# Gate and up projections as seven Strassen block products for eight, with the output and feed-forward stages arranged around them

## What is computed

```python
h = h + y @ w_out                                  # y: 1024 wide
hn = rmsnorm(h, norm_ffn_g)
gate, up = split(hn @ w_ffn_up)                    # 2 x 2816 features
gate = dwconv(gate, conv_ffn_w, conv_ffn_b)        # 3 taps over tokens t-1, t, t+1
h = h + (silu(gate) * up) @ w_ffn_down             # 2816 -> 1024
return h[16:]
```

## Time and profile before

| | us |
|---|---|
| median of 3 runs | 1465.31 |
| the profiled execution | 1464.26 |
| its span, first to last instruction | 1462.4 |
| input, recurrence, attention, first half of the output stage | 655.65 |
| second half of the output stage, to the first feed-forward matmul | 61.85 |
| feed-forward stage | 744.9 |
| one turn of the feed-forward loop | 66.74 |

### The profile page before, as it was taken

The page is one execution under the profiler, slowest core; times in us unless marked ns, Lnnn a source line. Parts: engine busy times, 40 slices in busy tenths (PEclk is TensorE's granted clock), DMA queues, the critical chain, the costliest instruction groups (busy, mean ns, idle before and its releaser), DMA issues.

```text
span 1462.4 us, 17247 instructions
## 1 busy us (share of the span) xinstructions
PE 1374.9 (94%) x6918; PEld 1150.0 (79%) x6918; DVE 728.3 (50%) x1002; ACT 527.3 (36%) x698; POOL 240.8 (16%) x133
## 2 busy tenths in 40 slices
PE   6989996799999987899799999999999999999998
PEld 5988995566666655587688989888888889898886
DVE  6767749577777751636333343424333332424243
ACT  6577624466666661525330212121111202121200
POOL 0000124000000000344221303122121213032100
PEclk9999899699999995899899999999999999999999
DMA  5101100000000032210120102021111102020103
GB/s 196 52 26 50 52 1 1 0 2 8 9 9 15 9 100 91 64 38 1 58 86 29 58 29 86 14 72 43 43 43 43 57 29 63 23 86 14 44 1 115
DMA packets 21094, 64.32 MB, mean 44 GB/s; under 512 B 5442, under 2 KB 6146, under 8 KB 18228
## 3 DMA queue, kind: packets, MB, share of 16 engines
q1 hardware_dynamic: 20676, 63.36, 12.7%
q10 hardware_dynamic: 368, 0.27, 0.1%
HBM read 59.20 MB, written 4.23 MB: 43 GB/s over the span
## 4 chain that ended last, share of the span: by engine, by line
PE 50%; DVE 0%; ACT 0%; issue 0%; DVEq 0%
PE banks L100 17%; PE banks L101 17%; PE banks L102 17%; DVE a_l L1867 0%; DVE ffn_act L1863 0%; ACT a_h L1829 0%; DVE h L1876 0%; DVEq L1862 0%
## 5 line engine op out<-in xcount | busy, mean ns | idle before, releaser
L100 PE MATMUL banks<-hn_h,up_h 128*128 128x342 f32 (+1 forms) x880 | 309.0, 351 | 1.7 <-PEq L1483 1.7
L101 PE MATMUL banks<-hn_l,up_h 128*128 128x342 f32 (+1 forms) x880 | 308.6, 351 | 0.0
L102 PE MATMUL banks<-hn_h,up_l 128*128 128x342 f32 (+1 forms) x880 | 308.0, 350 | 0.0
L100 PEld LDWEIGHTS banks<-hn_h,up_h 128*128 128x128 f32 x880 | 166.8, 190 | 17.1 <-POOL up_l L1509 1.8
L101 PEld LDWEIGHTS banks<-hn_l,up_h 128*128 128x128 f32 x880 | 167.1, 190 | 15.3
L102 PEld LDWEIGHTS banks<-hn_h,up_l 128*128 128x128 f32 x880 | 166.6, 189 | 15.6
L1876 DVE TENSOR_TENSOR h<-banks,h 128x512 f32<-128x512 f32 x176 | 121.7, 692 | 114.6 <-PE banks L102 114.6
L100 PE MATMUL banks<-dn_h,a_h 128*128 128x512 f32 x352 | 137.8, 392 | 3.7 <-DVE a_l L1867 3.7
L102 PE MATMUL banks<-dn_h,a_l 128*128 128x512 f32 x352 | 137.7, 391 | 0.0
L101 PE MATMUL banks<-dn_l,a_h 128*128 128x512 f32 x352 | 137.7, 391 | 0.0
L1794 POOL TENSOR_TENSOR dn_l<-dn_raw,dn_h 128x1024 fp32r<-128x1024 f32 x22 | 52.9, 2403 | 480.3 <-ACT dn_h L1827 480.3
(11 more groups left out here) (257 smaller groups left out, 2485.7 us busy)
## 6 DMA issues: line engine op xcount, KB each, us to landing
up_raw<-in_w_up SPq DMA_DIRECT2D x22, 1024.0 KB, 4.9
dn_raw<-in_w_down SPq DMA_DIRECT2D x22, 512.0 KB, 3.5
win_raw<-in_w_in SPq DMA_DIRECT2D x11, 512.0 KB, 3.3
x_tm<-in_x_tm SPq DMA_DIRECT2D x8, 512.0 KB, 4.4
wo_raw<-in_w_out SPq DMA_DIRECT2D x16, 256.0 KB, 4.7
h<-in_x_tm SPq DMA_DIRECT2D x8, 512.0 KB
out<-h SPq DMA_DIRECT2D x16, 256.0 KB, 2.0
sum_recip<-recip SPq DMA_DIRECT2D x7, 256.0 KB, 3.5
```

Of the source, the lines that this page charges most:

```text
L100: nc.tensor.matmul(out, w_h, x_h, start=first, stop=False)
L101: nc.tensor.matmul(out, w_h, x_l, start=False, stop=False)
L102: return nc.tensor.matmul(out, w_l, x_h, start=False, stop=last)
```

## The change

**Feed-forward.** The product of weights and hn is split once in each of its three dimensions: the output features of a group into its 2 tiles of 128, the 1024 contraction rows into 2 halves, the 1024 real tokens into 2 halves of 512. The eight block products of a gate pair, or an up pair, become seven by Winograd's form of Strassen's scheme. It needs four sums of weight blocks (S1 = A21 + A22, S2 = S1 - A11, S3 = A11 - A21, S4 = A12 - S2) and four sums of hn blocks (T1 to T4). The seven moving operands (`BLOCKS`) are made once, in the output stage; the weight sums are made in each group by VectorE, and each of the seven weight operands is split again into high (ScalarE) and low part (VectorE, before: GpSimd). A product accumulates over 4 contraction steps of 128, 12 matmuls of 512 columns; several products go on in one bank, and the four quadrants of the result come out as sums of banks: ScalarE copies one, VectorE adds the next. A group is now two units of 7 products: a = 0 the gate pair, a = 1 the up pair. The moving operand of a matmul is 4 pieces of 128 columns, one from each of four token-pair blocks (3584 words apart).

Up results are no longer read from the banks by the product; three quadrants go through `gs`, the fourth from its bank. The taps' first step moves to ScalarE, the other two stay on VectorE. The halo column of gate is computed apart: VectorE multiplies the raw gate weights by the meta token's hn and adds (8 steps per group), and two matmuls with a column of ones sum over partitions.

Down is cut in two halves of 8 units, one after each unit of the next group, over four banks (4 to 7) in place of three; token tiles 4 to 7 come first.

**Output stage, second half.** Tiles come in pairs (3, 7), (2, 6), (1, 5), (0, 4), then the meta tile. Each pair gives 7 blocks: three plain ones and four token sums made by VectorE from `hn`. They are transposed block by block (4 transposes each, into banks 4 to 7 in turn), between the matmuls of the units that follow, and split by ScalarE and VectorE. VectorE's list mixes bank sums, block splits, normalisation and token sums in a new order. The output projection's bank pairs are two instead of three there.

**Places.** Buffers move within SBUF, and 15 KB that were kept for descriptors are used. `w_ffn_up` is packed by blocks, one DMA of 256 KB per block.

The core of the diff (ScalarE's and VectorE's lists of a unit, and TensorE's):

```diff
+BLOCKS = ("b11", "b21", "b22", "t1", "t3", "t2", "t4")
...
+    second = [i for p in range(PAIRS - 1, -1, -1) for i in (p, p + PAIRS)] + [XT]
+    units = [(0, i) for i in [XT] + list(range(XT))] + [(1, i) for i in second]
...
+    def blocks_in(t):
+
+        if t < 2:
+            return []
+        if t > NT - 1:
+            return list(range(NBLK - 5, NBLK))
+        p, odd = divmod(t - 2, 2)
+        if odd:
+            return [NB * p + j for j in (2, 3, 4, 5)]
+        return ([NB * p - 1] if p else []) + [NB * p, NB * p + 1]
...
+            def token_sums(p):
+
+                a, b = hn
+                dve.wait_ge(sem["hn"], 2 * p + 2)
+                if p:
+                    dve.wait_ge(sem["hn_t"], NB * p)
+                nc.vector.tensor_tensor(tb[0], b[:, 0:half], a[:, 0:half], ALU.subtract).then_inc(sem["tok_sum"], 1)
+                dve.wait_ge(sem["tok_sum"], 4 * p + 1)
+                nc.vector.tensor_tensor(b[:, 0:half], b[:, half:], b[:, 0:half], ALU.subtract).then_inc(sem["tok_sum"], 1)
+                nc.vector.tensor_tensor(tb[1], b[:, half:], tb[0], ALU.subtract).then_inc(sem["tok_sum"], 1)
+                dve.wait_ge(sem["tok_sum"], 4 * p + 3)
+                nc.vector.tensor_tensor(tb[2], a[:, half:], tb[1], ALU.subtract).then_inc(sem["tok_sum"], 1)
...
+            for t in range(NT):
+                blocks = blocks_in(t + 1)
+                add_groups(NT + t)
+                early = 1 if t == NT - 2 else 2
+                for n in blocks[0:early]:
+                    low_h(n)
+                var_h(t)
+                for n in blocks[early:3 if early == 2 else 1]:
+                    low_h(n)
+                normalise(t)
+                if t % 2:
+                    token_sums(t // 2)
+                for n in blocks[3 if early == 2 else 1:]:
...
+                    if k % 2 and k // 2 < len(blocks):
+                        transpose_block(blocks[k // 2])
...
+    PRODUCTS = [(0, "b11", 0, True), (1, "t1", 2, True), (2, "t2", 0, False), (3, "b21", 3, True), (0, "t3", 0, False),
+                (3, "b22", 2, False), (2, "t4", 0, False)]
+    N_A11, N_S1, N_A12, N_S2, N_S3, N_A22, N_S4 = range(1, 8)
+    NEEDS = [N_A11, N_S1, N_S2, N_S2, N_S3, N_S4, N_S4]
+    P1, P5, P6, P2, P7, P3, P4 = range(1, 8)
+    SUM_S1, SUM_S3, SUM_S2, SUM_S4 = range(1, 5)
...
+            def unit(g, a, down=None, act_of=None, more=True):
+                if act_of is not None:
+                    for n in range(4):
+                        high_act(act_of, n)
+                high_s3(g, a)
+                if a:
+                    if not isinstance(g, int) or g:
+                        act.wait_ge(sem["conv2"], 2 * g + 2)
+                else:
+                    ready(act, "prod", 4 * g)
+                read(g, a, P1, 0, "11")
+                read(g, a, P5, 1, "22")
+                if a and isinstance(g, int) and g == 0:
+                    silu(g, 0)
+                    silu(g, 1)
+                high_a22(g, a)
+                read(g, a, P6, 2, "12")
+                if down is not None:
+                    high_down(down)
+                high_s4(g, a)
+                ng, na = (g, 1) if a == 0 else (g + 1, 0)
+                if more:
+                    high_a11(ng, na)
+                    high_s1(ng, na)
+                    high_a12(ng, na)
+                if a == 0:
+                    tap(g, 0)
+                    read(g, a, P4, 6, "21")
+                if more:
+                    high_s2(ng, na)
+                if a == 0:
+                    tap(g, 1)
+                    if not isinstance(g, int) or g:
+                        silu(g, 0)
+                        silu(g, 1)
...
+            def halo_part(g, c):
...
+                for k in range(4):
+                    x, s = blocks[:, :, P * k:P * k + P], halo[:, 4 * c + k:4 * c + k + 1]
...
+                        ins = nc.vector.scalar_tensor_tensor(out=hacc, in0=x, scalar=s, in1=hacc, op0=ALU.mult, op1=ALU.add)
...
+            def unit(g, a, act_of=None, down=None, more=True):
+                if act_of is not None:
+                    for n in range(4):
+                        low_act(act_of, n)
+                low_s3(g, a)
+                low_a22(g, a)
+                ng, na = (g, 1) if a == 0 else (g + 1, 0)
+                if more and na == 0:
+                    halo_part(ng, 0)
+                evacuate(g, a, P2, 3, "11")
+                if a:
+                    product(g, 0)
+                low_s4(g, a)
+                if more:
+                    low_a11(ng, na)
+                evacuate(g, a, P7, 4, "22")
+                if a:
+                    product(g, 1)
+                if more:
+                    sum_s1(ng, na)
+                    sum_s3(ng, na)
+                    sum_s2(ng, na)
+                    low_s1(ng, na)
+                evacuate(g, a, P3, 5, "12")
+                if a:
+                    product(g, 2)
+                if more:
+                    low_a12(ng, na)
+                if a == 0:
+                    sum_s4(ng, na)
+                    taps(g, 0, 1)
+                    add_some(down, (0,))
+                    taps(g, 0, 2)
+                    add_some(down, (1,))
+                    low_s2(ng, na)
+                    add_some(down, (2,))
+                    taps(g, 1, 1)
+                    add_some(down, (3,))
+                    taps(g, 1, 2)
+                    add_some(down, range(4, 8))
+                else:
+                    product(g, 3)
+                    add_some(down, (8,))
+                    if more:
+                        halo_part(ng, 1)
+                    add_some(down, (9,))
+                    if more:
+                        sum_s4(ng, na)
+                    add_some(down, (10,))
+                    if more:
+                        low_s2(ng, na)
+                    add_some(down, range(11, 16))
...
+            def unit(g, a):
+                for j, (slot, name, _, fresh) in enumerate(PRODUCTS):
+                    pe.wait_ge(sem["up_lo"], splits(g, a, NEEDS[j]))
+                    bank_free(g, a, j)
+                    o = acc(j, a).rearrange("p (i n) -> p i n", i=PAIRS)
+                    b = BLOCKS.index(name)
+                    for k in range(4):
+                        xs = [x[:, :, b, P * k:P * k + P] for x in (x_h, x_l)]
+                        terms = ((s_h, 0), (s_h, 1), (s_l, 0))
+                        for n, (s, w) in enumerate(terms):
+                            ins = nc.tensor.matmul(o, s[slot][:, k], xs[w], start=fresh and k == 0 and n == 0,
+                                                   stop=k == 3 and n == 2, skip_group_check=not fresh)
+                    ins.then_inc(sem["pr_mm"], 1)
+                    if a == 0 and j == 3:
+                        pe.wait_ge(sem["halo_sum"], 8 * g + 8)
+                        ready(pe, "prod", 4 * g)
+                        for m in range(2):
+                            ins = nc.tensor.matmul(bank(1)[:, 2 * m:2 * m + 2], hacc[:, m, :], ones[:, 0:2], start=True, stop=True)
+                        ins.then_inc(sem["halo_mm"], 1)
...
+            def down(g, s):
+                for n in range(8 * s, 8 * s + 8):
+                    if n == 0:
+                        pe.wait_ge(sem["dn_lo"], 2 * g + 2)
+                        pe.wait_ge(sem["a_lo"], 4 * g + 3)
+                    if n == 8:
+                        pe.wait_ge(sem["a_lo"], 4 * g + 4)
+                    i, c = TILES[n // 2], n % 2
                     ts, cs = slice(P * i, P * i + P), slice(512 * c, 512 * c + 512)
-                    if u >= 3:
-                        pe.wait_ge(sem["dn_read"], reads(g, u - 2))
+                    pe.wait_ge(sem["dn_read"], reads(g, max(n - 3, 0)))
                     for e in range(2):
-                        ins = split_products(nc, bank(5 + u % 3), a_h[e][:, ts], a_l[e][:, ts], dn_h[e][:, cs],
+                        ins = split_products(nc, bank(4 + n % 4), a_h[e][:, ts], a_l[e][:, ts], dn_h[e][:, cs],
                                              dn_l[e][:, cs], e == 0, e == 1)
                     ins.then_inc(sem["dn_mm"], 1)

+            def first(g):
+                unit(g, 0)
+                unit(g, 1)
+
             def group(g):
-                up(g, 0, False)
-                down(g - 1)
-                up(g, 1, False)
-
-            def first(g):
-                up(g, 0, True)
-                up(g, 1, False)
-
-            over_groups(pe, first, group, group)
```

727 lines of the change are left out of this document (478 added, 249 removed).

## The result

The changed kernel takes 1416.12 us (median of 4 runs, 1410.84 to 1417.38) where the one before takes 1464.68 (median of 4): a ratio of 0.9663, interval 0.9641 to 0.9685. The forecast was 1429. The profiled execution is the one of 1410.84, with a span of 1409.1 for 1462.4: 53.3 us less.

| stretch | before | after | change | forecast |
|---|---|---|---|---|
| up to the first bank sum of the output stage's second half | 655.92 | 649.45 | -6.5 | 0 |
| from there to the first feed-forward matmul | 61.58 | 72.23 | +10.7 | +20.3 |
| feed-forward stage | 744.9 | 687.4 | -57.5 | -56.3 |

A forecast was written before the change was run, and what follows sets the result against it. TensorE, busy 94% of the span, was taken to bound the kernel by number and length of matmuls. Feed-forward -59.8, its edges +3.5 and output stage +20.3 gave -36.0: 1429 us, own range 1417 to 1441, wide range 1408 to 1462.

The forecast's parts named there:

- The count of matmuls sets the turn: Feed-forward loop: TensorE's matmuls set each group's turn; ideal 60.1 us, 61.3 with waits, -59.8 over 11 groups.
- the step's bounds of 0 and 2.6: Feed-forward products: extra us a group if each of the moving operand's four pieces pays a fixed cost; 0 was taken.
- The waits: Feed-forward loop: TensorE waits 1.2 us a group, about 0.9 at down units, 0.3 at the up unit's sixth product.
- The lock: Feed-forward loop: VectorE splits wait out GpSimd's dn_l for whole instructions; sharing at half speed would save some 0.5 us a group.
- Edges of the stage: Feed-forward stage outside its 11 turns: late first products, group 0 and tail, together +3.5 us, bounds 0 and +8.
- The +3.0 of group 0: First feed-forward group, without a down half between its units: low weight splits 0.5, 1.6 and 0.8 us late.
- The output stage: Second half of that stage: VectorE's list sets pairs at 16.7 us; first feed-forward matmul at 735.3, +20.3 in all.
- The contention: Output stage's second half: GpSimd's y_l against VectorE's token sums and normalise, +1.5 us.
- 1 (VectorE's order sets the loop): Rival in the feed-forward loop: VectorE's in-order queue sets the pace, kernel slower, 1489 us; chance 0.11.
- 2: Rival in the feed-forward products: the moving operand in four pieces is slower, +29 us, 1458; chance 0.13.
- 3 (the output stage follows TensorE): Rival in the output stage: TensorE, not VectorE, sets the pairs, -9 us, 1420; chance 0.12.
- 4: Rival in the output stage: the clock falls in TensorE's gaps, as transposes don't count as busy, +21 us, 1450; chance 0.14.

The follow-up runs named there:

- experiment 5: Changed kernel with one contiguous 512-column moving operand, x_h's first quarter, for every feed-forward product, in place of four pieces: 1412.1 us.
- experiment 6: Changed kernel with one contiguous 512-column moving operand, x_l's last quarter, for every feed-forward product, in place of four pieces: 1409.95 us.
- experiment 4: Changed kernel with GpSimd's dn_l subtractions cut to 8 of 1024 columns, dn_h standing in for dn_l in the matmuls: 1416.05 us.
- experiment 8: Changed kernel with the four token sums per pair left out in the output stage's second half: 1409.56 us.
- experiment 3: Changed kernel with VectorE's split low_a11 of each gate unit done four times instead of once: 1453.03 us.
- experiment 10: The changed kernel run again, unaltered: 1416.78, 1417.95, 1415.90, 1411.39 and 1411.39 us, ratio 0.9663.
- experiments 6 and 9: Changed kernel, contiguous moving operand: x_l's last quarter in the one, 1409.95 us; eight places, x_h's quarters for gate and x_l's for up, in the other, 1416.48 us.

## Why the prediction was right, and where it was off

**The count of matmuls sets the turn: right.** 61.36 for 61.3, and putting an eighth product back gives 66.93. But that the number fits to 0.1 is luck: two errors cancel in it. The pitch of the products was to be 0.2267 and is 0.2323: +0.94 a turn, inside the step's bounds of 0 and 2.6; the four pieces, by which the upper bound was built, are not the cause (experiment 5). The earlier trace rows had the better figure, 0.2325 for up matmuls with hn as moving operand; the step took the output projection's instead. And the waits with the halo matmuls were to be 1.4 (1.2 and 0.2) and are 0.56: -0.84.

**The waits: size and place wrong.** Nothing waits at the down units. The step took low_a11 as 1.3 late; at 903.94 it begins as soon as its high part is there and takes 1.22 for 0.69, 0.53 late. The first down sum ends at 913.05, before the fifth down unit wants its bank at 914.14; the fourth is the tightest, 917.84 for 918.2. From the start of the gate unit the sum ends at 24.4 (near 25 in the step) and the bank is wanted at 25.5 (24.4 in the step): TensorE comes 1.1 later, of which 0.9 are there at the start of the down half (20.07 for 19.2), by its slower pace and the halo matmuls. So the two errors hang together. In experiment 6, whose pitch is nearly the forecast's, the turn has 0.99 beyond 264 matmuls of 0.2267 (60.84 less 59.85), and the stop before the last gate product costs 0.3 there, where it is 0.13 here. The 0.3 before the up unit's sixth product isn't there: the up unit has no stop. The only wait is before the gate unit's seventh product, for a bank read, and is 0.13 with its effects (experiment 4). The rest of the 0.56, 0.43, goes to the halo matmuls, 0.36 from start to start, and to the slower matmul behind them, where 0.2 was put. VectorE's 42.9 busy us are below the 44.5 of the sum.

**The lock.** A VectorE split beside a running GpSimd instruction took 1.53, then 1.22, where two back-to-back instructions of GpSimd took 5.20. VectorE did not wait for both to end: the split that began at 900.83 ended at 902.36, 0.55 behind the end of the first dn_l (899.41 and 2.40), and the one of 903.94 at 905.16, 0.55 behind that of the second (904.61). 0.55 is the split's own 0.69 less 0.14, as if each had run almost whole behind that end. Shared at half speed the first would have ended near 902.0. That agrees with the rule of the Trainium skill (SBUF — State Buffer, "SBUF: two separate sides") for one instruction; that the waiting engine then gets its turn between two is what the rows show, and GpSimd's second instruction, 2.85 for 2.40, fits that.

**Edges of the stage: +1.6 for +3.5.** 687.4 less 11 x 61.36 is 12.4, where before it was 10.8. The first product ran at half clock (matmuls 0.43 apart until 727.4), so the sums and splits that were to hold up the second were covered; TensorE waited 0.35 before the third. The +3.0 of group 0 shrinks to two waits of 0.22 (745.33) and 0.74 (760.23). Tail: 2.63 for the 2.9 forecast; the half clock behind it was to be shorter by 0.6, but eight matmuls start 0.43 apart (1382.80 to 1386.21), where before it were five (1436.43 to 1438.57).

**The output stage: the step that failed is the anchor.** The schedule of that half was laid from 661.30, the bank sums of the earlier trace rows, and its end compared with 717.50. But the half's first sums stand one unit earlier, at 655.92: the row at 661.30 is the second unit's. The change was so charged 5.4 us that both kernels pay. The schedule itself, 74.0 + 2.5 = 76.5 from its first sum, came out as 72.23: the way to the first pair took 17.56 for 15.6; the three pairs 16.99, 15.15 and 15.04 for 16.7, 16.7 and 16.4; the end 7.49 for 8.6. The contention is larger than the 1.5 put: four token sums are stretched by 0.9 to 1.0 each, 3.8 in all, and the 17.56 and the 10.50 contain it. Iterations that were put too long outweigh it: they are 6.49 and 8.66 without contention, where 7.2 and 9.5 were put. That VectorE sets this half is shown (experiment 8).

**The rivals.** 1 (VectorE's order sets the loop) would need 4.4 us of waits a turn; there are 0.13, though experiment 3 shows it to be a delay of one place away. 2 expected 0.242 from the four pieces; it is 0.2323, and one piece of x_h is no faster. 3 (the output stage follows TensorE): its time, 1420, is nearer than the forecast's, by the anchor and not by its mechanism. 4: the granted clock is 0.99 to 1.00 up to 714.19, with TensorE busy for only 12.11 of the 15.04 of the last pair; it falls in the end of the stage, as before. The rule on transposes that spoke for this rival changed nothing that a row shows.

**The 6.5 us ahead of the change** belong to no step. In the last attention head the granted clock fell to the 0.5 level some 5 us later in the profiled run after: by the means of the windows below at 548 before (0.80 over five us) and at 553 after (0.83 over the next five). The windows from 545 and 550 of the kernel before, then of the changed one:

```profile
545.00:550.00 5.00, 5.00 (x29) 4.32 (x28) 0.66 (x2) 1.94 (x2) 0.00 (x0) 0.80 1.04 419
550.00:555.00 5.00, 5.00 (x19) 4.46 (x20) 1.29 (x2) 0.00 (x0) 0.00 (x0) 0.50 1.02 408
```

```profile
545.00:550.00 5.00, 5.00 (x33) 4.33 (x33) 0.09 (x1) 1.94 (x2) 0.00 (x0) 1.00 1.03 417
550.00:555.00 5.00, 5.00 (x30) 4.63 (x29) 1.21 (x2) 1.31 (x2) 0.00 (x0) 0.83 1.00 399
```

That it is chance rests on experiment 10, where runs of one kernel have both values; only its profiled run shows when the clock fell. By its profiled execution, without that luck, the change is -47.4: -0.6 first half, +10.7, -57.5. The forecast's -36.0 is off by 11.4, of which 9.6 lie in the output stage.

## To carry to other kernels

Fix a schedule at the same instruction in both kernels before comparing ends: an anchor one unit late cost more than every duration in it. Where a second engine runs in time with the first, look for the place with the least slack; its idle time over a turn says nothing, since 2.1 us at the wrong place cost 3.7. Take an experiment for each term that is right only as part of a sum: pitch and waits were off by 0.94 and 0.84 a turn, with opposite signs, and a slower pace is itself cover for a late engine. Where two rows offer a price for the same matmul, as 0.2267 and 0.2325 here, ask which of the two has the same operand.

## Not expected of the hardware

Back-to-back matmuls of one shape have two paces at full granted clock: 0.2267 us (down, and x_l alone as moving operand in experiments 6 and 9) and 0.234 (x_h alone), with 0.2323 where both alternate. Contiguous or in four pieces makes no such difference, nor does the quarter of the buffer, nor does exchanging the two buffers' places.

It does not simply go with the operand and its values either. Against that stands dn_h, rounded high parts with 0.2267, and more so the output projection's second half, whose moving operand is the same before and after: 0.2267 before (from 654.97), 0.2323 after (48 matmuls in 11.15 us):

```profile
644.30 0.40 PE L100 MATMUL banks<-wo_h,y_h 128*128 128x512 f32 x1
...
655.45 0.40 PE L100 MATMUL banks<-wo_h,y_h 128*128 128x512 f32 x1
```

The change moved its high and low part in SBUF (from bytes 137184 and 153568 of a partition to 173504 and 96864), but also what runs beside it. So the place is not out, only its two simple forms are. What sets the pace stays open. It is worth 168 x 0.0056 = 0.94 us a turn, 10 us in the kernel.
